# A modulation row made in four column strips of TensorE and turned by a selector product, with its weights loaded ahead of the rows of x

## The reference, cut to what matters

```python
def modulation(cond, w_mod, b_mod):
    m = jnp.dot(jax.nn.silu(cond), w_mod) + b_mod
    return jnp.split(m, 3, axis=-1)
...
x = x + pos_embed_2d(n).astype(x.dtype)[None]
sh_x, sc_x, gt_x = modulation(c, w_mod[l], b_mod[l])
sh_c, sc_c, gt_c = modulation(c_ctx, w_mod[l], b_mod[l])
hx = rmsnorm(x, g_pre[l]) * (1 + sc_x[:, None, :]) + sh_x[:, None, :]
hc = rmsnorm(ctx, g_pre[l]) * (1 + sc_c) + sh_c
ux = jnp.einsum('bnd,de->bne', hx, w_in[l])
```

## Time and profile before

| | |
|---|---|
| median of 3 runs | 852.43 us (850.33 to 852.49) |
| the profiled execution | 854.36 us |
| its span in the trace | 852.3 us |
| PE busy | 771.0 us (90%) |
| DVE busy | 539.0 us (63%) |
| ACT busy | 456.3 us (54%) |
| POOL busy | 342.9 us (40%) |
| mean granted clock of PE | 0.953 |

### The profile page before, as it was taken

How to read it: one execution, slowest core, us unless ns; L and a number is a source line. 1 busy time by engine, 2 the same in 40 slices (tenths; PEclk the granted TensorE clock), 3 DMA queues, 4 the chain that set the end, 5 groups by cost and what they waited for, 6 DMA issues and landing times.

```text
span 852.3 us, 9918 instructions
## 1 busy us (share of the span) xinstructions
PE 771.0 (90%) x3468; PEld 616.6 (72%) x3468; DVE 539.0 (63%) x748; ACT 456.3 (54%) x749; POOL 342.9 (40%) x373
## 2 busy tenths in 40 slices
PE   6695899899889896999879997999999799999996
PEld 2275787688678785888758885777777488888885
DVE  4389763648866889399966554657615476666632
ACT  4264742697846963887944882343425243434311
POOL 0258653455544452535551466222210224242421
PEclk9797999999999997999998999899999999999998
DMA  9994014235424245234533234344337965857531
GB/s 365 357 302 152 25 38 126 59 90 164 146 74 144 77 145 159 94 116 145 168 108 105 68 101 145 90 132 137 111 111 277 302 211 176 273 171 261 178 124 77
DMA packets 89073, 130.09 MB, mean 153 GB/s; under 512 B 22752, under 2 KB 54112, under 8 KB 87488
## 3 DMA queue, kind: packets, MB, share of 16 engines
q1 hardware_dynamic: 84656, 115.44, 41.8%
q0 software_dynamic: 4368, 14.03, 6.2%
HBM read 91.17 MB, written 38.27 MB: 152 GB/s over the span
## 4 chain that ended last, share of the span: by engine, by line
PE 62%; DVE 11%; DMA 7%; ACT 6%; issue 5%; SPq 5%; POOL 4%; DVEq 0%; POOLq 0%; ACTq 0%
PE bank L1455 20%; PE bank L1456 19%; PE bank L1457 19%; SPq L418 2%; DMA scratch_u<-ustage 2%; DVE xc L1116 2%; PE bank L1483 1%; DMA wm<-in_w_mod 1%; DVE Qb L1262 1%; PE bank L1463 1%; DMA gb<-scratch_u 1%; DVE xTl L1167 1%; POOL spl L675 1%; DMA vbuf<-scratch_u 1%; DVE Ib L1252 1%
## 5 line engine op out<-in xcount | busy, mean ns | idle before, releaser
L1455 PE MATMUL bank<-xTh,wh 128*128 128x512 f32 (+1 forms) x592 | 235.0, 397 | 6.7 <-DVE wl L1142 4.1
L1457 PE MATMUL bank<-xTh,wl 128*128 128x512 f32 (+1 forms) x592 | 232.1, 392 | 0.0
L1456 PE MATMUL bank<-xTl,wh 128*128 128x512 f32 x576 | 228.4, 397 | 0.0
L1455 PEld LDWEIGHTS bank<-xTh,wh 128*128 128x128 f32 x592 | 114.3, 193 | 30.8 <-DVE wl L1142 4.7
L1457 PEld LDWEIGHTS bank<-xTh,wl 128*128 128x128 f32 x592 | 113.7, 192 | 24.0
L1456 PEld LDWEIGHTS bank<-xTl,wh 128*128 128x128 f32 x576 | 110.9, 192 | 23.1 <-issue 0.2
L1455 PE MATMUL bank<-xTh 128*128 128x512 f32 (+1 forms) x272 | 106.5, 391 | 13.6 <-DVE xTl L1400 7.1
L1457 PE MATMUL bank<-xTh,xTl 128*128 128x512 f32 x256 | 99.9, 390 | 0.0
L1456 PE MATMUL bank<-xTl,xTh 128*128 128x512 f32 x256 | 99.7, 390 | 0.0
L917 ACT ACTIVATE ustage<-bank 128x512 f32<-128x512 f32 x56 | 33.2, 594 | 117.2 <-PE bank L1457 101.7
L590 POOL TENSOR_SCALAR sph<-xc 128x512 fp32r<-128x512 f32 (+1 forms) x36 | 26.8, 760 | 118.7 <-PE bank L1457 88.6
(11 more groups left out here) (188 smaller groups left out, 1486.3 us busy)
## 6 DMA issues: line engine op xcount, KB each, us to landing
scratch_u<-ustage SPq DMA_DIRECT2D x72, 256.0 KB, 3.2
wraw<-in_w_in SPq DMA_DIRECT2D x18, 512.0 KB, 4.6
wm<-in_w_mod SPq DMA_DIRECT2D x8, 1024.0 KB, 11.7
xg<-in_x SPq DMA_DIRECT2D x16, 512.0 KB, 8.6
yb<-scratch_y SPq DMA_DIRECT2D x32, 256.0 KB, 3.0
gb<-scratch_u SPq DMA_DIRECT2D x32, 256.0 KB, 4.3
xres<-in_x SPq DMA_DIRECT2D x16, 512.0 KB, 4.8
out<-tout SPq DMA_DIRECT2D x16, 512.0 KB, 3.0
```

The lines of the kernel that those rows point to most:

```text
L1455: mm(out, wh_, xh_, start=first, stop=False)
L1456: mm(out, wh_, xl_, start=False, stop=False)
L1457: return mm(out, wl_, xh_, start=False, stop=last)
```

## The change

In words: (1) SP issues all eight pieces, with w_in tile 1 behind piece 5, before the rows of group 1, posr and posc. (2) `cs` is spread into `csw`, 32 columns for each k of which two are the conditions and 30 are zero; DVE clears and fills it. (3) The eight matmuls of a piece go to four strips of 32 columns, k modulo 4, so that the bank holds four partial sums in rows 0, 32, 64 and 96 (and the next ones), each of two matmuls. (4) DVE copies 128 rows of the bank instead of two. (5) The turn is a float32 matmul of the 128 by 128 block with `sel`, two columns that are 1 where the row modulo 32 is 0 or 1, which also sums the four strips. The queues of DVE, ACT, POOL and the rest of PE's keep their order.

```diff
--- before.py
+++ after.py
@@ -30,7 +30,7 @@
 _n = 0
 for _name, _w in (("c", 16), ("b_mod", 16), ("g_pre", 8), ("lru_ba", 8), ("lru_bx", 8), ("lam", 8),
                   ("conv_w", 16), ("conv_b", 4), ("pool_scale", 2), ("conf_dw_b", N_CONV),
-                  ("ln_g", 2), ("ln_b", 2), ("pool_edge", 32)):
+                  ("ln_g", 2), ("ln_b", 2), ("pool_edge", 32), ("sel", 2)):
     PAR[_name] = _n
     _n += _w
 N_PAR = _n
@@ -160,7 +160,8 @@
         posc = a2.take("posc", [P, CH])
         fbuf = a2.take("fbuf", [P, 4, CH])
         ident = a2.take("ident", [P, P])
-        mrow = a2.take("mrow", [2, 2 * D])
+        mrow = a2.take("mrow", [P, 2 * D])
+        csw = a2.take("csw", [P, KD, 32])
 
         a3 = Area(r0, end)
         xc = a3.take("xc", [P, CTX + SEQ])
@@ -267,6 +268,7 @@
 
         s_par, s_id, s_posc = sem("params_in"), sem("ident_ready"), sem("poscol_in")
         s_wm = [sem(f"wmod_in{m}") for m in range(8)]
+        s_csw = sem("padded_c")
         s_mrow, s_modT = sem("mod_rows"), sem("mod_turned")
         s_cs, s_mod, s_sc, s_kl = sem("silu_c"), sem("mod_psum"), sem("scales_ready"), sem("lru_consts")
         s_xin = [sem(f"x_in{g}") for g in range(NCH + 1)]
@@ -439,12 +441,11 @@
                     load_w(0)
                 if m == 1:
                     load_rows(0)
-                if m == 3:
+                if m == 5:
                     load_w(1)
-                if m == 5:
-                    load_rows(1)
-                    load_pos(1)
-                    sp.dma_start(posc[:], pos_col).then_inc(s_posc, 16)
+            load_rows(1)
+            load_pos(1)
+            sp.dma_start(posc[:], pos_col).then_inc(s_posc, 16)
             load_w(2)
             load_rows(2)
             load_pos(2)
@@ -1115,6 +1116,10 @@
             def stt(out, in0, sc, in1, op0, op1):
                 return v.scalar_tensor_tensor(out=out, in0=in0, scalar=sc, in1=in1, op0=op0, op1=op1)
 
+            v.memset(csw[:], 0.0).then_inc(s_csw, 1)
+            dve.wait_ge(s_csw, 1)
+            dve.wait_ge(s_cs, 1)
+            v.tensor_copy(csw[:, :, 0:2], cs.rearrange("p (k s) -> p k s", s=2)).then_inc(s_csw, 1)
             v.memset(epsc, EPS).then_inc(s_kl, 1)
             v.memset(lnepsc, LN_EPS).then_inc(s_kl, 1)
 
@@ -1171,7 +1176,7 @@
 
                 for m in blocks:
                     dve.wait_ge(s_mod, 2 * m + 2)
-                    v.tensor_copy(mrow[:, m * CH:(m + 1) * CH], bank[4 + m][0:2, :]).then_inc(s_mrow, 1)
+                    v.tensor_copy(mrow[:, m * CH:(m + 1) * CH], bank[4 + m][:]).then_inc(s_mrow, 1)
 
             def scales():
 
@@ -1456,19 +1461,20 @@
                 mm(out, wh_, xl_, start=False, stop=False)
                 return mm(out, wl_, xh_, start=False, stop=last)
 
-            pe.wait_ge(s_cs, 1)
+            pe.wait_ge(s_csw, 2)
             for m in range(8):
                 pe.wait_ge(s_wm[m], 16)
                 for k in range(KD):
-                    ins = mm(bank[4 + m // 2][0:2, (m % 2) * 256:(m % 2) * 256 + 256], cs[:, 2 * k:2 * k + 2],
-                             wm[:, m, k, :], start=(k == 0), stop=(k == KD - 1))
+                    strip = slice(32 * (k % 4), 32 * (k % 4) + 32)
+                    ins = mm(bank[4 + m // 2][strip, (m % 2) * 256:(m % 2) * 256 + 256], csw[:, k, :], wm[:, m, k, :],
+                             start=(k < 4), stop=(k >= 4))
                 ins.then_inc(s_mod, 1)
-            pe.wait_ge(s_id, 2)
+            pe.wait_ge(s_par, 16)
             for m in range(4):
                 pe.wait_ge(s_mrow, m + 1)
                 for j in range(4):
                     mt = 4 * m + j
-                    ins = nc.tensor.transpose(bank[0][:, 2 * mt:2 * mt + 2], mrow[:, mt * P:(mt + 1) * P], ident[0:2, 0:2])
+                    ins = mm(bank[0][:, 2 * mt:2 * mt + 2], mrow[:, mt * P:(mt + 1) * P], par_col("sel", 0, 2), start=True, stop=True)
                 ins.then_inc(s_modT, 1)
 
             def transposes(gi, ks=range(KD)):
@@ -1676,7 +1682,8 @@
         cols(a["lru_lambda"][0]), cols(a["lru_conv_w"][0].reshape(4, N_LRU, P).transpose(1, 0, 2)),
         cols(a["lru_conv_b"][0]), cols(a["pool_scale"][0]),
         np.repeat(a["conf_dw_b"][0].reshape(N_CONV, GROUP_CH), PHASES, axis=1).T,
-        cols(a["conf_ln_g"][0]), cols(a["conf_ln_b"][0]), pool_edges()], axis=1)
+        cols(a["conf_ln_g"][0]), cols(a["conf_ln_b"][0]), pool_edges(),
+        np.eye(32, 2, dtype=np.float32)[np.arange(P) % 32]], axis=1)
 
     gw = np.stack([a["lru_wa"][0], a["lru_wx"][0]], axis=1)
     gw = gw.reshape(2, 2, N_LRU, 2, 64, 64).transpose(2, 3, 4, 0, 1, 5).reshape(N_LRU, P, 4, 64)
```

## The result

The changed kernel took 858.35 to 862.92 us in three runs (862.92, 858.35, 860.33; the median is 860.33), the kernel before a median of 851.88 beside them. The ratio of the two is 1.0103, with an interval of 1.0083 to 1.0123, or 8.8 us more. A fourth execution, 1086.69 us at a mean granted clock of 0.671, is left out. The profiled execution has a span of 861.1 us, against 852.3.

The account below looks back on a forecast made before the run. Two paths, PE's modulation row and DVE's rows of x, were taken to bound the start together. Order of loads +5.0 and turn +2.4 made 7.4 us on the median 852.4: 859.8 us, range 855.8 to 862.2.

Parts of the forecast that it names:

- The sum's two terms: Delay of `scales`: 5.0 us from the order of loads plus 2.4 from the turn, 7.4 us in all.
- The bound: Start of the kernel: PE's modulation row and DVE's path for the rows of x arrive within 0.55 us of one another.
- Part 1, the loads, +5.0: SP's order of loads: group 1's rows, posr and posc land behind two pieces; +5.0 us, range 4.7 to 5.3.
- Parts 2 and 3, nothing: Strip matmuls on PE, and DVE's csw and 128-row copies: worth nothing; row done at 31.4 or 37.9, copies 1.27 a pair.
- Part 4, the turn, +2.4: PE's turn behind the last copies: 4.2 us to `scales` in place of 1.76, +2.4 us, range +0.4 to +4.4.
- the transposes' price: Turn's 16 records priced as 128 by 128 transposes at the half clock: 3.42 us.
- the upper bound, with no overlap: PE's turn with weight loads of 0.334 us each, not overlapped: 5.3, 6.2 us in all, +4.4.
- the 2.5 us: Turn's records by the skill's weight-load rule: old 0.078 each, 0.156 at half clock, 2.5 us instead of 3.42.
- One for one to the end: From `scales` to the kernel's end: a shift of `scales` carries through whole.
- Rows of x no later: Rival on DMA: row loads and posc land at 35.7 as before; 852.8 to 854.8 us; chance 10%.
- The early row decides: Rival at the start: row ready at 31.4 lets ACT modulate at 36.9, about 839 us; 4% with other unforeseen gains.
- PE at the half clock and one strip at a time: Rival on PE's strips: 128 records end at 69.0, up to 17 us behind the copies, 877 us; chance 4%.

Follow-up runs that it names:

- the control: Kernel before, with 16 matmuls that feed nothing put ahead of piece 6 on PE: 851.55 us, ratio 0.9996.
- the strips alone: Changed kernel with SP's old order of loads, keeping the strips, 128-row copies and selector turn: 855.27 us, ratio 1.0042 to the kernel before.
- The loads alone: Kernel before with SP's new order of loads and nothing else: 855.98 us, ratio 1.0051.
- the busy PE: Changed kernel with 34 matmuls that feed nothing between PE's second and third turn: 858.90 us, ratio 1.0087 to the kernel before.
- the pure delays: Kernel before with 9, then 13 chained DVE sums that feed nothing ahead of `scales`: 859.27 us (1.0082) and 861.37 us (1.0107).
- the context group first: Changed kernel with the row's copies, `scales` and context rows' work ahead of group 1 in the engines' queues: 853.38 us, 1.0019 to the kernel before.
- the context group first and PE kept busy: Changed kernel with context rows' work queued ahead of group 1, plus 45 matmuls that feed nothing in PE's waits: 851.18 us, 0.9994 to the kernel before.

## Why the prediction came out as it did

**The number.** The forecast was 859.8 us, 7.4 more than before; the median was 860.33, 8.8 more by the ratio. That the time came closer than the difference is luck: the kernel before had 851.88 beside these runs, not the 852.43 that I started from. The sum's two terms, at `scales`, came out as 6.3 and 2.6 for 5.0 and 2.4, the second inside its range, the first above its upper bound of 5.3.

**The bound.** That two paths arrived together at 46.8 and 47.4, and that shortening PE's would give nothing, is shown twice with the old order of loads, by the control and by the strips alone. The loads alone show that a row ready early waits for DVE's queue.

**Part 1, the loads, +5.0.** The mechanism was right: the rows of x and posc go behind two pieces, DVE's queue has the copies behind them, and PE's finished row waits. It alone cost 4.3 us at the end and 6.2 at `scales`. The term was sized too small, 5.0 for 6.3. Pieces 6 and 7 moved as bytes say (30.5 for 30.4), but posc came 6.3 us later in the profiled execution and 4.6 to 6.3 in the six traces with this order. "The engines are never idle in this, so a new order only exchanges places" is the step that was too simple: the places are exchanged, the rates are not kept.

**Parts 2 and 3, nothing.** The row was done at 32.5 and the copies cost the same 1.28. Right, for the reason given, the cover by DVE's path. The working had the matmuls' price from a mean over both clocks, 0.243 a record, where 3.54/16 = 0.221 is that of the full one; nothing hangs on it.

**Part 4, the turn, +2.4.** It measured 2.59 (4.35 for 1.76), with 3.57 for the 16 records where I took 3.42, from transposes at the half clock. The choice between the prices rested on the clock, and the busy PE shows that it was the right ground: 1.84 at the full one. That the transposes' price came so near is in part luck, as they move 128 columns and these records 2. The reason given for them, that float32 weight loads are recorded longer, held in kind and was misread in size: the 334 ns of the earlier trace rows stand from 677.4 us on, where the granted clock is 0.50 (0.54 on the mean from 678 to 681), and I held them against 136 and 141 ns at the full one. At the same clock the loads of the new turn were recorded at 192 ns with PE kept busy, for the old turn's 136, and at 333 in the changed kernel, for 219 with the loads alone. They overlapped, one every 0.223 us, so the upper bound, with no overlap, was far off.

The Trainium skill's rule on weight loads ("TensorE: Matmul & The Clock Gate", LDWEIGHTS (loading the stationary operand)) says that rows don't count, and no run here contradicts that. But the 2.5 us that I worked out from it took the old turn's 0.078 for a record of any kind: a record of the float32 matmul takes 1.84/16 = 0.115 us at the full clock, though both load 128 columns. (The 1.20 us of the earlier trace rows over 16 records is 0.075, not 0.078; that changes little.) Whether the kind of the instruction or its 128 rows make the difference, these two don't separate; the transposes' own loads, 136 ns with two rows and 141 with 128, speak for the kind.

**One for one to the end.** It held for the pure delays (5.7 to 7.0, 9.05 to 9.1) and for the changed kernel (8.87 to 8.8). Over all eleven experiments time and start differ by -1.9 to +2.9 us, 0.6 on the mean. Part of this is that the start is read from one execution and the time from others. Within the thirteen traces, from DVE's sums of group 2 to the end of the span took 786.2 us (the loads alone) to 791.3 (the context group first), and 790.6 before. What makes these differ is open. That scatter was not in the prediction, which took only the runs' own spread.

**The rivals.** Rows of x no later: excluded by every trace. The early row decides: excluded as the queue stood, and then made true by reordering it, where `scales` came at 35.4 as against the 35.6 that this rival reckons (31.4 + 4.2). Its 839 us were wrong even so: group 1's rows come at 40 to 42 and set everything behind the context rows. In that trace the sums of group 2 start at 62.34, no earlier than before, and the time was 853.4. PE at the half clock and one strip at a time: half of it came, the half clock, but side by side a piece takes 1.94 and stays ahead of its loads at 2.5.

## What to carry to other kernels

Before you make one input of a joint early, look at the others: a chain of waits names the one that ended last, and here the second stood 0.55 us behind it, in the same DMA queue and ahead in the same engine's queue. Moving a load forward moves others back by about the time of its bytes (here 4.6 to 6.3 us for 5.0 reckoned), and an engine whose queue is in order turns that into a wait for work that was ready. When a step is made fast, move its consumer up too. Here that was worth 7 us against the changed kernel and left it 1.6 us over the kernel before; in the old queues the fast step was worth nothing, and in the new ones its worth was not measured.

## What was not expected of the hardware

Before, PE went through pieces 0 to 5 without a pause, and its trace records the clock's rise to 1.00 at 11.8 us and its fall at 32.3, after the end of them. With the strips PE waits for every piece. In the changed kernel they start 2.5 to 5.0 us apart, PE is busy for 1.07 to 1.94 us with each, and the clock was at the full level for one of them only: pieces 0 to 3 took 1.93 or 1.94 us each, piece 5 took 1.07, and from 25.2 us on the granted clock is 0.50, so that the last pieces, turns and transposes are done at 1.2 GHz until beyond 60 us. With the strips alone all eight pieces took 1.93 or 1.94. (Until the first change that a trace records, at 54.0 us in that one, the profile's clock column shows 1.00; there the durations tell the level.) With the context group first and PE kept busy, pieces 2 to 7 took 1.07 each.

So the faster form of a matmul slowed its successors: with the strips alone, a turn's 16 records took 3.57 and 3.58 us, in the changed kernel with PE kept busy 1.84. In the changed kernel itself this added nothing on the path, since PE would have stood idle before the last turn anyway; with the loads alone, without strips, the granted clock was 0.50 at the turn too. The matmuls that feed nothing gave 1.3 us at `scales` in the changed kernel, and 1.6 with the context group first.
